# One more step of lag in three attention loops, and ScalarE's tables loaded ahead of them

## The reference

```python
# diff_attention (8 heads of 2 x 64): scores for two components, chunk mask of 64
sc = einsum('bqhcd,bkhcd->bhcqk', qb, k) * scale
p = masked_softmax(sc, chunk_mask(blk, s))
a = p[:, :, 0] - lam * p[:, :, 1]
o = einsum('bhqk,bkhe->bqhe', a, v)          # then rms_norm(o, subln_g) * (1 - lambda_init)
# mla_attention (16 heads, 64 + 32 for scores, 64 for values), same mask
# _windowed_gqa (16 heads over 4 key heads, 64): window of 128, a bias, a sink logit in the softmax
```

## Time and profile before

| what | us |
|---|---|
| median of 3 runs (lowest, highest) | 2805.05 (2804.94, 2809.26) |
| the profiled execution, its own time | 2810.7 |
| its span, first to last instruction | 2808.9 |
| TensorE busy (share) | 2599.7 (93%) |
| VectorE busy | 1797.4 (64%) |
| ScalarE busy | 1301.2 (46%) |
| GpSimd busy | 778.8 (28%) |
| mean granted TensorE clock, of full | 0.963 |

### The profile page before, as it was taken

How to read it: one execution, slowest core, us unless ns; L and a number is a source line. 1 busy time by engine, 2 the same in 40 slices (tenths; PEclk the granted TensorE clock), 3 DMA queues, 4 the chain that set the end, 5 groups by cost and what they waited for, 6 DMA issues and landing times.

```text
span 2808.9 us, 47348 instructions
## 1 busy us (share of the span) xinstructions
PE 2599.7 (93%) x15959; PEld 2332.8 (83%) x15959; DVE 1797.4 (64%) x3387; ACT 1301.2 (46%) x1915; POOL 778.8 (28%) x786
## 2 busy tenths in 40 slices
PE   7779987899899988999999999779888999999998
PEld 5669875699799877899999998679787899999997
DVE  5668745678556998555555555557998555555555
ACT  4556544655444155444444444454165444444443
POOL 0200002100000201355555555130101355555554
PEclk9989998899999999999999999889999999999999
DMA  5135642256555412666666665414413566666664
GB/s 185 52 106 172 187 127 67 85 171 183 168 165 166 128 38 88 189 181 187 185 187 186 186 187 178 129 53 143 135 38 103 185 187 183 187 186 187 186 185 144
DMA packets 170078, 420.43 MB, mean 150 GB/s; under 512 B 13968, under 2 KB 66637, under 8 KB 169726
## 3 DMA queue, kind: packets, MB, share of 16 engines
q1 hardware_dynamic: 162894, 412.82, 48.4%
q10 hardware_dynamic: 7088, 6.33, 0.7%
HBM read 418.02 MB, written 1.08 MB: 149 GB/s over the span
## 4 chain that ended last, share of the span: by engine, by line
PE 76%; DVE 16%; issue 3%; ACT 2%; POOL 2%; DVEq 1%; SPq 0%; ACTq 0%; DMA 0%; POOLq 0%
PE PS L447 24%; PE PS L449 24%; PE PS L448 24%; DVE oh L1884 4%; DVE oh L1881 1%; POOL arena L1967 1%; DVE lo L1334 1%; DVE arena L1847 1%; DVE arena L1469 1%; DVE arena L1479 1%; DVE arena L1851 1%; DVEq L1884 1%; DVE arena L1781 1%; DVE arena L1785 1%; DVE arena L1782 1%
## 5 line engine op out<-in xcount | busy, mean ns | idle before, releaser
L1334 DVE TENSOR_TENSOR lo<-raw,hi 128x1024 fp32r<-128x1024 f32 x732 | 1007.7, 1381 | 779.7 <-ACT hi L908 778.0
L908 ACT ACTIVATE hi<-raw 128x1024 fp32r<-128x1024 f32 x732 | 765.8, 1054 | 503.1 <-PE PS L449 486.3
L447 PE MATMUL PS<-xh,hi 128*128 128x256 f32 x2784 | 791.7, 284 | 2.6 <-DVE xl L1382 2.6
L448 PE MATMUL PS<-xl,hi 128*128 128x256 f32 x2784 | 791.4, 284 | 0.0
L449 PE MATMUL PS<-xh,lo 128*128 128x256 f32 x2784 | 791.2, 284 | 0.0
L447 PEld LDWEIGHTS PS<-xh,hi 128*128 128x128 f32 x2784 | 537.6, 193 | 12.9 <-issue 4.1
L448 PEld LDWEIGHTS PS<-xl,hi 128*128 128x128 f32 x2784 | 537.8, 193 | 8.0
L449 PEld LDWEIGHTS PS<-xh,lo 128*128 128x128 f32 x2784 | 537.4, 193 | 0.0
L447 PE MATMUL PS<-hi,Ah 128*128 128x512 f32 x1024 | 404.0, 395 | 10.8 <-DVE lo L1334 7.1
L449 PE MATMUL PS<-hi,Al 128*128 128x512 f32 x1024 | 404.6, 395 | 0.0
L448 PE MATMUL PS<-lo,Ah 128*128 128x512 f32 x1024 | 404.2, 395 | 0.0
(11 more groups left out here) (222 smaller groups left out, 3007.2 us busy)
## 6 DMA issues: line engine op xcount, KB each, us to landing
raw<-in_peer_u SPq DMA_DIRECT2D x256, 512.0 KB, 3.6
raw<-in_peer_v SPq DMA_DIRECT2D x256, 512.0 KB, 4.4
raw<-in_ffn_w_up SPq DMA_DIRECT2D x88, 512.0 KB, 3.6
raw<-in_ffn_w_down SPq DMA_DIRECT2D x44, 512.0 KB, 4.2
raw<-in_peer_w_q SPq DMA_DIRECT2D x32, 512.0 KB, 4.4
raw<-in_da_w_qkv SPq DMA_DIRECT2D x24, 512.0 KB, 3.9
raw<-in_conv_w_in SPq DMA_DIRECT2D x24, 512.0 KB, 3.6
raw<-in_attn_w_qkv SPq DMA_DIRECT2D x12, 512.0 KB, 4.3
```

The costliest lines, as they stand in the source:

```text
L447: pe.matmul(o, ah, bh, start=start, stop=False)
L448: pe.matmul(o, ah, bl, start=False, stop=False)
L908: cp.activation(hi[:, s, 0:size], raw[:, s, 0:size], ACT.Copy).then_inc(hi_made, 1)
L1334: V.tensor_tensor(lo[:, s, 0:size], raw[:, s, 0:size], hi[:, s, 0:size].bitcast(F32), ALU.subtract).then_inc(lo_made, 1)
```

## The change

The lag between `largest(s)` and `begin(s)` grows by a step, and with it all that follows it: `begin` and `finish` go from step s + 2 to s + 3, turn and `probs` from s + 3 to s + 4, values from s + 5 to s + 6, `head_out` from odd steps (2h + 7) to even ones (2h + 8), the squares from 2h + 8 to 2h + 9. Each loop gets one step more. In da the rotation of banks takes in bank 4. A dummy Exp stands ahead of ScalarE's loop in all three attentions, and in da a dummy Sqrt in step 20, behind the last `probs`. Nothing changes on GpSimd and SyncE, and no transfer is touched.

```diff
@@ TensorE attention @@
                 def bank():
                     count[0] += 1
-                    return 5 + count[0] % 3
+                    return 4 + count[0] % 4 if a is da else 5 + count[0] % 3
...
-                for s in range(a.nsub + 5):
+                for s in range(a.nsub + 6):
...
-                    if 0 <= s - 3 < a.nsub:
-                        turn_weights(s - 3)
-                    if s == 5:
+                    if 0 <= s - 4 < a.nsub:
+                        turn_weights(s - 4)
+                    if s == 6:
...
-                    if s >= 5:
-                        values(s - 5)
+                    if s >= 6:
+                        values(s - 6)
@@ ScalarE attention @@
-                for s in range(a.nsub + (8 if a is da else 4)):
+                cp.activation(small[:, 58:59], ss[:, 4:5], ACT.Exp, scale=0.0)
+                for s in range(a.nsub + (9 if a is da else 5)):
...
-                    if 0 <= s - 3 < a.nsub:
-                        probs(s - 3)
-                    if a is da and s % 2 == 0 and 0 <= s - 8 < a.nsub:
-                        h = (s - 8) // 2
+                    if 0 <= s - 4 < a.nsub:
+                        probs(s - 4)
+                    if a is da and s == a.nsub + 4:
+                        cp.activation(small[:, 58:59], ss[:, 4:5], ACT.Sqrt)
+                    if a is da and s % 2 == 1 and 0 <= s - 9 < a.nsub:
+                        h = (s - 9) // 2
@@ VectorE attention @@
-                for s in range(a.nsub + (6 if a is da else 2)):
+                for s in range(a.nsub + (7 if a is da else 3)):
...
-                    if 0 <= s - 2 < a.nsub:
-                        begin(s - 2)
+                    if 0 <= s - 3 < a.nsub:
+                        begin(s - 3)
                     if s < a.nsub:
                         largest(s)
-                    if 0 <= s - 2 < a.nsub:
-                        finish(s - 2)
-                    if a is da and s % 2 == 1 and s >= 7:
-                        head_out((s - 7) // 2)
+                    if 0 <= s - 3 < a.nsub:
+                        finish(s - 3)
+                    if a is da and s % 2 == 0 and s >= 8:
+                        head_out((s - 8) // 2)
```

## The result

The changed kernel takes 2784.85 us (median of 4 runs, 2779.5 to 2787.55) beside 2807.16 for the kernel before on the same chip; the ratio is 0.9914, 95% interval [0.9902, 0.9926]. The forecast was 2784.0. The profiled span went from 2808.9 to 2782.3 us.

What follows compares the result with a forecast made beforehand. It took each attention loop to be bound by a cycle of waits, no engine being full; -9.7 (da) - 4.0 (mla) - 7.2 (gqa) = -20.9 us from the median 2805.05 gave 2784, range 2777 to 2796.

Steps and rivals of the forecast that it cites:

- rivals 1 to 4: Only da gains, 2795, chance 0.18; more waits go, 2778, 0.08; port conflict, 2806, 0.06; slower TensorE clock, 2818, 0.04.
- The short cycle: All three loops: largest(s), double(s), plus_one(s-1), begin(s-1), largest(s+1), a round trip per step; the lag spreads it over two.
- signs of being wrong: A da loop above 58 us, mla steps below 2.7, or begin medians well over 0.56 (port right).
- da, -9.7: First attention loop: waits removed, less start, ScalarE's bound, drain and table load, sum -9.7 us; two steps at 5.96.
- -12.3 + 0.6 + 1.0: da: 12.3 us of waits go; begin(0) still waits 0.6; ScalarE's pace in the first eight steps costs 1.0.
- mla, -4.0: Second attention loop: start -3.0, table load -0.5, steps 14 and 15 -1.2, drain +0.7; steps 7 to 13 unchanged.
- The load's -0.5: mla: the Exp table load sits in a 6.64 us ScalarE wait and frees 0.5 us.
- gqa, -7.2: Third attention loop: load +1.5, first steps -1.8, steps 2 to 7 -5.4, steps 7 to 15 -2.2, drain +0.7.
- The bank cycle of 6.54: gqa: chain from largest through turn, values and scores, 6.54 us per two steps, 8.25 at the low clock.
- The drains: Loop ends: extra work behind the last largest, costed at +0.6 us in da, +0.7 in mla and gqa.
- The port: VectorE and GpSimd hinder each other: 0 to some 0.22 us per meeting for VectorE, 0.3 in gqa; 0.7 taken there.
- rival 3: begin(s-2) may not run beside plus_one(s-1): gain 0, loads cost 1.3 us, time 2806; chance 0.06.

Runs made afterwards that it cites:

- GpSimd's order alone: Kernel before, lags unchanged; in da alone GpSimd runs plus_one(s) ahead of double(s+1): ratio 0.9977.
- probs first alone: Kernel before with its two-step lag; in mla and gqa ScalarE's probs(s-3) moved ahead of Exp and Tanh of step s: ratio 0.9988.
- bank only: Kernel before with four banks instead of three in da's ring, nothing else: ratio 1.0006.
- With probs first: Changed kernel; in mla and gqa ScalarE's probs(s-4) moved ahead of Exp and Tanh of step s: ratio 0.9868 to the kernel before.
- the order in all loops and no lag: Kernel before, its lag kept, with GpSimd's plus_one ahead of the next double in all three loops and four banks in da: ratio 0.9924.

## Why the prediction was right

The result lies 0.85 us from the forecast and inside its own range, 2779 to 2790; rivals 1 to 4 fall. That closeness is partly luck. The three loops gave 24.1 us for a forecast of 20.9, with da outside its own range of -8 to -11. The forecast took 5.65 us off because the profile before was that much above its median; the profile after, 2784.15, is 0.7 below its own, and the median before moved to 2807.16 with a fourth run, so that the medians differ by 22.3. The mechanism is right. By its own steps:

- **The short cycle** is shown by the experiments: GpSimd's order alone takes it out of da's steady part, probs first alone meets it in mla (5.81), and in gqa its wait stands under another engine's name. The text had the cycle right and, in its reading of the waits, took over that name. Of its signs of being wrong none came: its da loop of 63.0 us is the window of 51.0 now, not above 58, mla's steps are 2.94, and da's `begin` still takes 0.56 or less.
- **da, -9.7, measured -11.9.** Two steps take 5.87 (5.96 forecast), `begin` waits 0.4. From `largest(0)` to `largest(15)` it is 47.67 to 35.73 us, -11.94, where -12.3 + 0.6 + 1.0 gave -10.7. The drain, costed at +0.6, took 20.16 instead of 20.51. The first `largest` comes 0.42 later, for 0.35. The bank was named as needed and given no price; it is 1.3 to 2.6, all in the start.
- **mla, -4.0, measured -4.1,** out of terms that missed in both directions. Steps 7 to 13: 5.88 for two and a gain of 0, as forecast. Steps 2 to 7 gave -2.3 for -3.0, steps 14 and 15 -1.0 for -1.2, the drain -0.8 for +0.7. The load's -0.5 is there, between `largest(0)` and `largest(2)`. The first `largest` came 0.6 later, which had no term. The first scores start 2.59 us into the loop in both kernels, but their matmuls took 0.42 to 0.63 us each at the clock's lower level in the changed kernel, and 0.28 to 0.38 in the kernel before. One profile with the old mla (bank only) shows the same 0.42 to 0.63, and two with the new one do not, so that is scatter.
- **gqa, -7.2, measured -8.2.** First scores +1.5 for +1.5 (the load and its small activation take 1.5 by their rows, of which the run without them gave back 0.6); the first two steps -1.0 for -1.8; steps 2 to 7 -4.9 for -5.4; steps 7 to 15 -3.6 for -2.2, of which 0.7 is the price of the port, which was not paid; the drain -0.1 for +0.7. The bank cycle of 6.54 is seen as 6.60, the low one of 8.25 as 7.45 and 7.81, twice instead of once, and the last pair takes 5.26.
- **The drains** are the one term wrong in all three: three `begin`/`finish` pairs behind the last `largest` were costed at +0.6 to +0.7 and cost nothing (-0.4, -0.8 and -0.1).
- **The port.** `begin` in gqa took 0.71 us on average before and 0.70 after, so VectorE paid next to nothing: one `begin` took 1.02 us, as one did before, and one `finish` 0.98, the others 0.69. By the rule of the Trainium skill (SBUF — State Buffer, "Who interferes with whom"), as rival 3 priced it, the time would have been 2806. The cost fell on GpSimd: twelve of its sixteen `plus_one` in gqa took 1.90 to 1.91 us instead of 1.49, and their mean went from 1.49 us to

```profile
L1970 POOL TENSOR_SCALAR arena<-arena 128x512 f32<-128x512 f32 x16 | 28.8, 1801 | 0.0
```

With the lag in place this was off the path.

What stays open: why TensorE's granted clock drops twice in gqa. With probs first its waits for `probs` ahead of the turns are gone (6.0 us in four in the changed kernel) and from 1800 us to the last `largest` the clock stays up; that the one brings the other was not tried by itself. The kernel with the order in all loops and no lag speaks against so simple a cause: it has 5.5 us of these waits, in four too, and its clock is 1.00 from 1814 us to its last `largest`.

## What to carry over

Where an idle engine appears at the head of the longest wait, write down the order of its own queue first: here two swapped GpSimd instructions, with a fourth bank in one loop, gave nearly what an extra pipeline step gave. Two cycles of equal length hide each other: the two cures were worth 1.5 and 4.1 us in mla by themselves and 10.5 together, so cost an edit against the next cycle, and try the pair. A cure for a cycle that no longer binds can be one itself: measure it on top, don't add it on trust.

## What was not expected of the hardware

Issuing a transfer held ScalarE's queue for 0.71 us (nine in 6.43), so transfers issued at the head of a loop cost gqa 3.5 us of its start and 4.9 of its stretch. VectorE and GpSimd meeting in memory lengthened GpSimd's instruction by 0.31 us on average (1.49 to 1.80) and VectorE's seldom: in gqa two of 32 by 0.3 us, the others not at all. `double`, of two columns, took 0.60 us in gqa while a `finish` ran and 0.21 to 0.27 apart from it.
